# A two-layer hybrid trunk on one core: order of exponents, products and weight splits in the second mixer, and of ScalarE's first instructions

## The reference

```python
g = jax.nn.log_sigmoid((z_lr @ w_gate_up + b_gate).astype(jnp.float32)) / GLA_GATE_TAU
...
def step(state, inp):
    qj, kj, vj, bj = inp
    diff = bj[:, :, :, None, :] - bj[:, :, None, :, :]
    decay = jnp.exp(jnp.where(causal[:, :, None], diff, -jnp.inf))
    attn = jnp.einsum('bhtk,bhsk,bhtsk->bhts', qj, kj, decay)
    o = jnp.einsum('bhts,bhsv->bhtv', attn, vj) + \
        jnp.einsum('bhtk,bhkv->bhtv', qj * jnp.exp(bj), state)
...
o = o * lax.rsqrt(jnp.mean(o * o, axis=-1, keepdims=True) + EPS) * g_norm.astype(jnp.float32)
o = o * jax.nn.silu(r.astype(jnp.float32)).reshape(B, S, H, DV)
```

## Time and profile before

| | |
|---|---|
| median of three runs | 1238.08 us |
| time of the profiled execution | 1240.42 us |
| its span | 1238.7 us |
| TensorE busy | 1202.3 us, 97% |
| VectorE busy | 614.3 us, 50% |
| ScalarE busy | 456.4 us, 37% |
| GpSimd busy | 41.7 us, 3% |
| TensorE's share of the chain that ended last | 94% |
| DMA engines busy, first and second of 40 slices of the span | 8 tenths, 2 tenths |
| mean granted clock | 0.993 |

### The profile page before, as it was taken

How to read it: one execution, slowest core, us unless ns; L and a number is a source line. 1 busy time by engine, 2 the same in 40 slices (tenths; PEclk the granted TensorE clock), 3 DMA queues, 4 the chain that set the end, 5 groups by cost and what they waited for, 6 DMA issues and landing times.

```text
span 1238.7 us, 14642 instructions
## 1 busy us (share of the span) xinstructions
PE 1202.3 (97%) x5821; PEld 1006.4 (81%) x5821; DVE 614.3 (50%) x838; ACT 456.4 (37%) x711; POOL 41.7 (3%) x88
## 2 busy tenths in 40 slices
PE   5999999999999999999998999999999999999996
PEld 4788888888888888888878887987888888888885
DVE  5437887645334344353446675484542443433432
ACT  5346666544224123133253324142631231321321
POOL 2000000000000000000020101100000000000001
PEclk9999999999999999999999999999999999999998
DMA  8236655523223332223311230132233332233001
GB/s 258 60 89 160 145 128 154 178 95 114 93 100 102 102 102 90 91 91 102 102 37 35 69 102 18 51 101 104 85 102 102 102 102 97 75 99 102 34 0 68
DMA packets 115991, 119.00 MB, mean 96 GB/s; under 512 B 38913, under 2 KB 84001, under 8 KB 115938
## 3 DMA queue, kind: packets, MB, share of 16 engines
q1 hardware_dynamic: 112992, 116.47, 30.9%
q10 hardware_dynamic: 2946, 1.79, 0.5%
HBM read 103.50 MB, written 2.10 MB: 85 GB/s over the span
## 4 chain that ended last, share of the span: by engine, by line
PE 94%; DVE 2%; ACT 1%; issue 1%; ACTq 1%; SPq 0%; POOL 0%; DMA 0%; POOLq 0%; DVEq 0%
PE bank L885 15%; PE bank L888 15%; PE bank L889 15%; PE bank L872 9%; PE bank L875 9%; PE bank L876 9%; PE bank L1059 2%; PE bank L1063 2%; PE bank L1062 2%; PE bank L1229 2%; PE bank L1107 2%; PE bank L1094 1%; PE bank L1180 1%; PE bank L1184 1%; PE bank L1183 1%
## 5 line engine op out<-in xcount | busy, mean ns | idle before, releaser
L1422 DVE TENSOR_TENSOR w_lo<-w_stage,w_hi 128x2048 fp32r<-128x2048 f32 x87 | 199.9, 2300 | 214.0 <-ACT w_hi L561 214.0
L561 ACT ACTIVATE w_hi<-w_stage 128x2048 fp32r<-128x2048 f32 x87 | 166.0, 1911 | 267.4 <-PE bank L885 213.4
L872 PE MATMUL bank<-hT_lo,w_hi 128*128 128x512 f32 x512 | 200.0, 391 | 0.0
L876 PE MATMUL bank<-hT_hi,w_lo 128*128 128x512 f32 x512 | 199.5, 390 | 0.0
L885 PE MATMUL bank<-w_lo,u_hi 128*128 128x512 f32 x512 | 199.5, 390 | 0.0
L875 PE MATMUL bank<-hT_hi,w_hi 128*128 128x512 f32 x512 | 199.4, 389 | 0.0
L889 PE MATMUL bank<-w_hi,u_lo 128*128 128x512 f32 x512 | 199.4, 389 | 0.0
L888 PE MATMUL bank<-w_hi,u_hi 128*128 128x512 f32 x512 | 199.4, 389 | 0.0
L885 PE MATMUL bank<-w_lo,hT_hi 128*128 128x512 f32 (+1 forms) x320 | 116.1, 363 | 3.8 <-DVE hT_lo L1713 1.9
L1496 DVE TENSOR_TENSOR u_sq<-relu 128x512 f32<-128x512 f32 x64 | 44.3, 692 | 143.3 <-ACT relu L618 143.3
L618 ACT ACTIVATE relu<-bank 128x512 f32<-128x512 f32 x64 | 38.3, 599 | 205.3 <-PE bank L876 205.3
(11 more groups left out here) (205 smaller groups left out, 1522.4 us busy)
## 6 DMA issues: line engine op xcount, KB each, us to landing
w_stage<-in_mlp_w_up_dram SPq DMA_DIRECT2D x32, 1024.0 KB, 5.1
w_stage<-in_mlp_w_down_dram SPq DMA_DIRECT2D x32, 1024.0 KB, 5.0
w_stage<-in_fox_w_in_dram SPq DMA_DIRECT2D x32, 256.0 KB, 4.1
w_stage<-in_gla_w_in_dram SPq DMA_DIRECT2D x8, 1024.0 KB, 5.1
w_stage<-in_fox_w_in_dram SPq DMA_DIRECT2D x4, 1024.0 KB, 8.8
qa<-qk_hi SPq DMA_DIRECT2D x32, 128.0 KB
w_stage<-in_fox_w_out_dram SPq DMA_DIRECT2D x4, 1024.0 KB, 5.2
w_stage<-in_gla_w_in_dram SPq DMA_DIRECT2D x8, 512.0 KB, 4.2
```

Source lines behind the costliest of these rows:

```text
L561: act.activation(w_hi[:, slot, :], w_stage[:, slot, :], ACT.Copy).then_inc(w_hi_made, 1)
L872: a = pe.matmul(out, w[0][:, k, :], x[1][:, k, :], start=(k == 0), stop=False)
L876: a = pe.matmul(out, w[1][:, k, :], x[0][:, k, :], start=False, stop=(k == KT - 1))
L1422: dve.tensor_tensor(w_lo[:, slot, :], w_stage[:, slot, :], fp(w_hi[:, slot, :]), ALU.subtract).then_inc(w_lo_made, 1)
```

## The change

Four things are changed; nothing that is computed changes.

- ScalarE's four small DMAs at the start are issued after the eight `hT_hi` of the first norm, ahead of the split of weight unit 1. In their place stands a square of one column of the identity into a new scratch tile `warm`, which waits for the identity, and with which the load of the activation table comes first.
- Heads 0 and 2 of the second mixer, ScalarE: `decays` of one more level stands ahead of each weight split.
- Heads 0 and 2, VectorE: each `split_lo` stands one to three steps later.
- Head 3: on both engines the splits of units c + 12 to c + 14 stand later, the `tanhs` are cut in two with an exponent between, and differences and products stand ahead of `keep_goT`.

```diff
@@ scalar, start
-            act.dma_start(gn, gla_norm_g.rearrange("a (j p) -> (a p) j", p=P),
-                          allow_slow_non_contiguous=True).then_inc(gn_loaded, 16)
-            act.dma_start(bf_col[:], fox_b_f.rearrange("a h -> h a"), allow_slow_non_contiguous=True).then_inc(bf_loaded, 16)
-            act.dma_start(gate_w[:, 0, :, :], fox_in_d[:, :, 3 * D:3 * D + FOX_H]).then_inc(gate_w_loaded, 16)
-            act.dma_start(gate_w[:, 1, :, :],
-                          gla_in_d[:, :, 2 * GLA_K + D:2 * GLA_K + D + RANK]).then_inc(gate_w_loaded, 16)
+            act.wait_ge(ident_made, 1)
+            act.activation(warm, ident[:, 0:1], ACT.Square).then_inc(warmed, 1)
...
             norm(0)
+            act.dma_start(gn, gla_norm_g.rearrange("a (j p) -> (a p) j", p=P),
+                          allow_slow_non_contiguous=True).then_inc(gn_loaded, 16)
+            act.dma_start(bf_col[:], fox_b_f.rearrange("a h -> h a"), allow_slow_non_contiguous=True).then_inc(bf_loaded, 16)
+            act.dma_start(gate_w[:, 0, :, :], fox_in_d[:, :, 3 * D:3 * D + FOX_H]).then_inc(gate_w_loaded, 16)
+            act.dma_start(gate_w[:, 1, :, :],
+                          gla_in_d[:, :, 2 * GLA_K + D:2 * GLA_K + D + RANK]).then_inc(gate_w_loaded, 16)
             split_hi(0, 0, 1)
             act.wait_ge(gate_w_loaded, 32)
@@ scalar, head 0
             decays(0, 2)
+            decays(0, 3)
             keep_v(0, 3)
             split_hi(0, 0, c + 4)
-            decays(0, 3)
             decays(0, 4)
+            decays(0, 5)
             turn_tail(0)
             split_hi(0, 0, c + 5)
-            decays(0, 5)
             decays(0, 6)
+            decays(0, 7)
             split_hi(0, 0, c + 6)
-            decays(0, 7)
@@ scalar, head 2
             decays(2, 4)
+            decays(2, 5)
             turn_tail(2)
             split_hi(0, 0, c + 10)
-            decays(2, 5)
             decays(2, 6)
+            decays(2, 7)
             split_hi(0, 0, c + 11)
-            decays(2, 7)
@@ scalar, head 3
             decays(3, 2)
+            decays(3, 3)
             split_hi(0, 0, c + 12)
-            decays(3, 3)
-            tanhs(3)
+            decays(3, 4)
+            tanhs(3, (0, 1))
+            decays(3, 5)
+            tanhs(3, (2, 3))
             keep_goT(0)
             keep_goT(1)
-            decays(3, 4)
+            decays(3, 6)
             keep_goT(2)
             keep_goT(3)
             turn_tail(3)
-            decays(3, 5)
-            split_hi(0, 0, c + 13)
             keep_goT(4)
             keep_goT(5)
-            decays(3, 6)
             decays(3, 7)
+            split_hi(0, 0, c + 13)
             split_hi(0, 0, c + 14)
@@ vector, head 0
             keep(0, 1)
-            split_lo(0, 0, c + 4)
             differences(0, 4)
             decayed(0, 3)
             keep(0, 2)
             differences(0, 5)
             decayed(0, 4)
+            split_lo(0, 0, c + 4)
             keep(0, 3)
-            split_lo(0, 0, c + 5)
             differences(0, 6)
             decayed(0, 5)
             keep(0, 4)
             differences(0, 7)
             decayed(0, 6)
+            split_lo(0, 0, c + 5)
             keep(0, 5)
-            split_lo(0, 0, c + 6)
             states(0)
             decayed(0, 7)
+            split_lo(0, 0, c + 6)
@@ vector, head 2
             keep(2, 3)
-            split_lo(0, 0, c + 10)
             differences(2, 6)
             decayed(2, 5)
             keep(2, 4)
             differences(2, 7)
             decayed(2, 6)
+            split_lo(0, 0, c + 10)
             keep(2, 5)
             states(2)
-            split_lo(0, 0, c + 11)
             decayed(2, 7)
             keep_qk(3)
+            split_lo(0, 0, c + 11)
@@ vector, head 3
             decayed(3, 2)
-            split_lo(0, 0, c + 12)
             keep(3, 1)
             differences(3, 4)
             decayed(3, 3)
+            split_lo(0, 0, c + 12)
             keep(3, 2)
+            differences(3, 5)
+            decayed(3, 4)
             silus(3)
+            differences(3, 6)
             keep_goT(0)
             keep_goT(1)
-            differences(3, 5)
-            decayed(3, 4)
             keep(3, 3)
+            decayed(3, 5)
             keep_goT(2)
             keep_goT(3)
-            differences(3, 6)
-            decayed(3, 5)
-            split_lo(0, 0, c + 13)
             keep(3, 4)
+            differences(3, 7)
+            decayed(3, 6)
             keep_goT(4)
             keep_goT(5)
...
```

More of the change, by code:

```diff
@@ L180, in fox_gla_trunk @@
         gn = sb("gn", [P, 8])[:, 0:2]
-        turn = sb("turn", [1, 16])[:, 0:1]
+        turn = sb("turn", [1, 8])[:, 0:1]
+        warm = sb("warm", [P, 8])[:, 0:1]
         with ExitStack() as mem:
@@ L250, in fox_gla_trunk @@
         gate_hi_made, gate_lo_made, f_summed = sem("gate_hi_made"), sem("gate_lo_made"), sem("f_summed")
-        pool_step, ident_made, fox_consts_made = sem("pool_step"), sem("ident_made"), sem("fox_consts_made")
+        pool_step, ident_made, fox_consts_made, warmed = (
+            sem("pool_step"), sem("ident_made"), sem("fox_consts_made"), sem("warmed"))
         gla_filled, xor_filled, xor_made, xor_cut, masks_made = (
@@ L739, in decays, with tanhs @@
                 act.activation(decay[:, lv % 2, :], decay[:, lv % 2, :], ACT.Exp, scale=1.0 / TAU).then_inc(decay_made, 1)
-            def tanhs(a):
+            def tanhs(a, ts=range(TB)):
                 act.wait_ge(grstd_made, 1)
@@ L745, in tanhs @@
                     act.wait_ge(go_made, a * TB)
-                for t in range(TB):
+                for t in ts:
                     act.wait_ge(r_done, a * 2 + t // 2 + 1)
@@ L1831, in _ @@
             decayed(3, 3)
+            split_lo(0, 0, c + 12)
             keep(3, 2)
+            differences(3, 5)
+            decayed(3, 4)
             silus(3)
+            differences(3, 6)
             keep_goT(0)
             keep_goT(1)
-            differences(3, 5)
-            decayed(3, 4)
             keep(3, 3)
+            decayed(3, 5)
             keep_goT(2)
             keep_goT(3)
-            differences(3, 6)
-            decayed(3, 5)
-            split_lo(0, 0, c + 13)
             keep(3, 4)
+            differences(3, 7)
+            decayed(3, 6)
             keep_goT(4)
             keep_goT(5)
-            differences(3, 7)
-            decayed(3, 6)
             keep(3, 5)
+            decayed(3, 7)
             states(3)
-            decayed(3, 7)
+            split_lo(0, 0, c + 13)
+            keep(3, 6)
             split_lo(0, 0, c + 14)
-            keep(3, 6)
             keep(3, 7)
```

## The result

The changed kernel takes 1224.62 us, the median of four runs (1224.22 to 1224.86). The kernel before takes 1239.22 us beside it (four runs, 1237.83 to 1240.52). The ratio is 0.9884, with a 95% interval of 0.9871 to 0.9896: 14.6 us less, where 1226.7 us was forecast. The profiled execution took 1224.22 us, against 1240.42 before, 16.2 us less.

A forecast was written before the change was run, and what follows sets the result against it. TensorE was taken as the bound, busy 1202.3 of 1238.7 us. Gains 2.5 + 4.6 + 2.4 + 0.5 + 3.4 = 13.4 from 1240.42 gave 1227.0; median-based 1228.1 and 1226.4 led to 1226.7, range 1223.0 to 1231.5.

The forecast's parts named there:

- Start: Kernel start: moving four DMAs and the table load ahead lets ScalarE's squares end earlier, 2.5 us gained (0 to 3.3).
- the hold by the late quarters of x: Kernel start: the third square waits for late x data, at most until 8.7; without that hold the gain is 3.3 us.
- The moved DMAs: ScalarE after the eight high halves: four issues at 20.6 take 2.1 us; cost 0, at worst 0.1 us.
- The rule weighed against it: Gate weights: issue DMAs early, wait late; speaks against the move, exposing the whole wait; prediction expected only ScalarE to feel it.
- Rivals 2 and 4: 2: gate weights land late for ScalarE, 1236.7 us, chance 0.05; 4: start does not move, 1229.5 us, chance 0.08.
- rival 3: ScalarE before unit 1's split: moved issues hold it 29.2 us, TensorE waits 24.4, time 1251.4 us; chance 0.02.
- Head 0: Second mixer: TensorE's waits at levels 3 and 5 go, 2.31 + 2.28 = 4.6 us gained; later splits have cover.
- head 2: Second mixer: TensorE's wait at level 5 goes, 2.4 us gained.
- Head 3: Second mixer: third transpose's wait grows to 1.5 us, repaid by earlier level products; net 0.5 us gained (-0.5 to 1.2).
- Clock: TensorE in the second mixer: slow stretches after the waits at 670 and 772 go, 3.4 us gained (0 to 5.1).
- Rival 1: Waits go but the low clock moves, likely behind head 3's wait or at 848: 1228.7 to 1230.4 us, chance 0.2.
- The sum: Whole kernel: all gains total 13.4 us, taken from the profiled 1240.42 us, giving 1227.0 us.

The follow-up runs named there:

- experiment 1: Kernel before plus only the start's edits (four DMAs moved, one-column warm-up square), second mixer as before: 1235.36 us, ratio 0.9974.
- experiment 3: Kernel before plus the one-column warm-up square first, the four small DMAs left ahead of the squares: 1237.32 us, ratio 0.9993.
- experiment 4: Kernel before plus the four DMAs moved, without the warm-up square, second mixer as before: 1235.62 us, ratio 0.9982.
- 6: Kernel before plus only ScalarE's edits of heads 0 and 2, VectorE as before: 1238.7 us, ratio 1.0006.
- 9: Kernel before plus only VectorE's edits of heads 0 and 2, ScalarE as before: 1228.14 us, ratio 0.9909.
- experiment 7: Kernel before plus only head 3's edits, on both engines: 1238.49 us, ratio 0.9998.
- 2: Kernel before plus all second-mixer edits, the start as before: 1228.78 us, ratio 0.9921.
- 8: Changed kernel with TensorE's last early output-projection block moved behind the last two transposes: 1222.05 us, ratio 0.9874 to the kernel before.
- 11: Changed kernel with VectorE's level 6 difference and unit c + 12 low half moved behind goT 0 and 1 low halves in head 3: 1224.72 us.
- 5: Kernel before plus only head 0's edits, on both engines: 1232.89 us, ratio 0.9956.
- 10: Kernel before plus only head 2's edits, on both engines: 1235.16 us, ratio 0.9975.

## Why the prediction was right, point by point

The time was 1224.62 where 1226.7 was forecast, in the range, and faster as expected. By its steps:

- **Start, 2.5 us (0 to 3.3).** Mis-sized by 0.5: 3.0 at equal clock (experiment 1) and between the means of the profiles. The mechanism was right, with issues that held the squares (3) and a table load that needs nothing (4). What was mis-sized is the hold by the late quarters of x: the third square began at 8.09, 0.40 us of waiting, not at 8.7, so the transposes began 3.08 earlier. The 4.25 of the pair has 1.17 on top, for the transposes themselves were faster in this execution, as the rows of single transposes show (min/median/max ns; two stretches of after, then all of before's to 19.4 us):

```profile
L937 PE MATMUL bank<-ident,hn x13: 273/421/476, 10.4 to 13.0; 128*128 128x128 f32 x13
...
L937 PE MATMUL bank<-ident,hn x19: 272/273/408, 12.6 to 14.7; 128*128 128x128 f32 x19
```

```profile
L932 PE MATMUL bank<-ident,hn x28: 325/418/474, 13.5 to 19.3; 128*128 128x128 f32 x28
```

  They fall to 273 ns 2.6 us after the first in the one and not within 5.8 us in the other, while the granted clock reads 1.00 in both. When they fall differs from execution to execution, whatever the start: the 29 transposes take 4.86 to 6.25 us in the seven profiles with the old start and 4.56 to 6.03 in the six with the new. The means, 5.6 and 5.3, differ by less than that scatter, so the 1.17 us is chance.
- **The moved DMAs, cost 0.** Right in the sum, wrong in the working. The issues were put behind the eight high halves, at 20.6 with 2.1 us in which ScalarE stands. They ran at 15.02 to 17.68, beside the high halves, and took 2.57 together, while ScalarE went on with the activations that stand ahead of them. Unit 1's split began at 18.83, and TensorE never asked for it in vain.
- **The rule weighed against it.** The gate weights landed 7.7 us after issue at the most, not 12.1, and ScalarE waited 3.57 us for them. The rule of "DMA: Bandwidth & Descriptors" (Trainium skill, table of rules) named the right wait, and the trace shows it on ScalarE alone: TensorE has no wait between 18 and 46 us. By the rule the change should have lost there, and the measurement decides against it for this place. Rivals 2 and 4 did not occur, nor did rival 3: the longest of the four issues took 1.03 us.
- **Head 0, 4.6 us, and head 2, 2.4 us.** Right, and by the books some 0.17 us per stop came on top. What the prediction did not see is which half does it: it named both the exponent behind ScalarE's split and VectorE's own split, and only the second one counted (6 and 9). The splits' later low halves cost nothing, as said.
- **Head 3, 0.5 us (-0.5 to 1.2).** Mis-sized low: 1.12 in the profile, 1.13 in experiment 7. The wait at the third transpose came as forecast (1.61, said 1.5). All three kl waits of the head went, 1.33 us by the trace of before. Counted from the head's start, level 5 came 0.45 us earlier (21.12 to 20.67), the gain forecast; level 6 then brought another 0.52, its own wait of 0.30 and the rest of level 5's stop, which the prediction named but did not count. Of the 1.12 us, the idle time of TensorE's matmuls shows 0.28, and the rest fits what a stop costs beyond its length: TensorE's weight loads, which run ahead of the matmuls, waited 3.7 us in the head before and 2.6 after.
- **Clock, 3.4 us.** Right in the pair: two of three stretches went, the one behind the last head stayed. That this was worth the full 3.4 is luck of the profiled execution. Among the seven profiles that have the waits, half clock followed the wait at 670 in three and the one at 772 in six, so on average an estimated (3/7 + 6/7) x 1.7 = 2.2 us. Rival 1, that the low clock moves to the new wait in head 3, is not seen behind that wait in the profiles of the changed kernel or of experiments 2, 7 and 8. Its wider form, that another stretch may appear, happened in experiments 2, 4 and 11, behind the 0.87 us wait at 637 (0.5 for 6.8 us).
- **The sum, 13.4 from the profiled 1240.42.** Measured 16.2: 1.75 more from the start, 0.6 from head 3, 0.5 left over at the mixer's three stops. The median moved 14.6 beside its own four runs of before, and 13.8 against the larger sets. The sizes found above, with the average for the clock, give the same: 3.0 + 7.0 + 0.5 + 1.1 + 2.2 = 13.8. The forecast of 1226.7 was 2.1 us too high, and the terms for the start, head 3 and the three stops are where it was short.

## What to carry to other kernels

When a long piece of filler work (here a weight split) stands on two engines ahead of a short product that TensorE wants, look first at the second engine: it both waits for the filler's first half and then spends its own, and moving that one entry may be all that is needed. Put many small DMA issues behind the first work of a start, not ahead of it; the table load then needs no warm-up. Shorten the last waits of TensorE even where they are under 2 us, since the half clock that may follow costs nearly as much again (1.7 us behind a wait of 1.88, in eight of twelve profiles). And do not size a term from one pair of profiles: this one showed 4.25 us at the start, where six and seven profiles give 3.0.

## What the runs showed of the hardware

- A wait decides the clock only in part. In the profiles, the 1.88 us wait behind the last head was followed by half clock before, in the changed kernel and in experiments 1, 3, 5, 6, 7 and 10, but not in 2, 4, 9 and 11. Each of the three long mixer waits stands in seven profiles: the one of 2.31 us at 670 had it in three (before, 4, 7), the one of 2.28 at 682 in none, the one of 2.41 at 772 in six (all but 5). The new wait of 1.6 us in head 3 had none in four profiles, the one of 0.87 at 637 had one in 2, 4 and 11, out of fourteen. The stretches were 3.41 us long, those behind the 0.87 us wait 6.83. What picks them was not found.
- DMA issues on ScalarE's queue ran beside activations that stood ahead of them (15.02 to 17.68), so the order of the code is not kept there, but held those behind them (experiment 3, 7.61). The same four issues took 2.6 us at 15 us and 4.9 from 2.91 on before, when x and the first weights were in flight.
- The table load took 1.28 us in every profile, and stood ahead of the wait for x in experiment 4 as well (3.31, the square at 5.76). By the Trainium skill, "ScalarE: Activation LUTs", in the section on what the load costs, it takes about 1.28 us, the same for every set; the trace agrees.
